# Two of the four weight sums of each feed-forward Strassen block made by accumulating DMA, and a third such block in ten of the eleven gate/up pairs

## What is computed

```python
def swiglu(h, w_gate, w_up, w_down):
    return (jax.nn.silu(h @ w_gate) * (h @ w_up)) @ w_down   # D_FF = 5632
x = x + swiglu(rmsnorm(x, norm_ffn_g), w_ffn_gate, w_ffn_up, w_ffn_down)
return rmsnorm(x, norm_final_g)
```

## Time and profile before

| | us |
|---|---|
| median of 3 runs | 1755.81 |
| lowest and highest | 1754.05, 1756.22 |
| the profiled execution, its time | 1754.56 |
| its span, first to last instruction | 1752.2 |
| feed-forward part, from about | 1035 |

### The profile page before, as it was taken

How to read it: one execution, slowest core, us unless ns; L and a number is a source line. 1 busy time by engine, 2 the same in 40 slices (tenths; PEclk the granted TensorE clock), 3 DMA queues, 4 the chain that set the end, 5 groups by cost and what they waited for, 6 DMA issues and landing times.

```text
span 1752.2 us, 20308 instructions
## 1 busy us (share of the span) xinstructions
PE 1740.3 (99%) x7926; PEld 1444.7 (82%) x7926; DVE 1283.2 (73%) x1399; ACT 972.8 (56%) x1209; POOL 28.4 (2%) x54
## 2 busy tenths in 40 slices
PE   9999999999999999999999999999999999999998
PEld 7888888888888888888888888888888888888886
DVE  7577677887575757655565578888888788888787
ACT  6767678554555555544455465555545545555554
POOL 1000000000000000000000000000000000000000
PEclk9999999999999999999999999999999999999999
DMA  8565665666565655556755455566666565666664
GB/s 284 173 200 167 204 193 162 199 204 204 163 209 168 216 168 189 172 186 209 249 184 189 138 177 181 192 194 194 196 209 207 184 209 192 192 192 194 215 202 158
DMA packets 176047, 338.22 MB, mean 193 GB/s; under 512 B 10704, under 2 KB 15312, under 8 KB 175696
## 3 DMA queue, kind: packets, MB, share of 16 engines
q1 hardware_dynamic: 173232, 327.72, 59.3%
q0 software_dynamic: 1296, 5.24, 0.9%
q10 hardware_dynamic: 1424, 3.97, 0.6%
HBM read 334.80 MB, written 2.10 MB: 192 GB/s over the span
## 4 chain that ended last, share of the span: by engine, by line
PE 97%; DVE 1%; ACT 0%; DMA 0%; issue 0%; ACTq 0%; DVEq 0%; POOLq 0%; POOL 0%
PE group L468 29%; PE group L470 29%; PE group L469 29%; PE side L468 2%; PE side L469 2%; PE side L470 2%; PE side L531 2%; DVE w_lo L1199 0%; DMA x_T_in<-in_x_T 0%; PE side L649 0%; PE side L633 0%; PE side L587 0%; PE side L586 0%; PE side L585 0%; DVE x_res L1551 0%
## 5 line engine op out<-in xcount | busy, mean ns | idle before, releaser
L817 ACT ACTIVATE w_hi<-w_raw 128x1024 fp32r<-128x1024 f32 x612 | 622.9, 1029 | 543.5 <-PE group L470 447.9
L1199 DVE TENSOR_TENSOR w_lo<-w_raw,w_hi 128x1024 fp32r<-128x1024 f32 x612 | 712.6, 1186 | 286.3 <-ACT w_hi L817 280.3
L468 PE MATMUL group<-w_hi,x_hi 128*128 128x512 f32 x1466 | 575.6, 393 | 0.5 <-DVE w_lo L1274 0.3
L470 PE MATMUL group<-w_hi,x_lo 128*128 128x512 f32 x1466 | 571.0, 390 | 0.0
L469 PE MATMUL group<-w_lo,x_hi 128*128 128x512 f32 x1466 | 570.5, 389 | 0.0
L468 PEld LDWEIGHTS group<-w_hi,x_hi 128*128 128x128 f32 x1466 | 275.3, 188 | 58.9 <-DVE w_lo L1199 2.0
L470 PEld LDWEIGHTS group<-w_hi,x_lo 128*128 128x128 f32 x1466 | 275.1, 188 | 57.9
L469 PEld LDWEIGHTS group<-w_lo,x_hi 128*128 128x128 f32 x1466 | 275.4, 188 | 55.6
L817 ACT ACTIVATE w_hi<-w_sums 128x1024 fp32r<-128x1024 f32 x84 | 89.1, 1061 | 148.1 <-PE group L470 107.2
L1199 DVE TENSOR_TENSOR w_lo<-w_sums,w_hi 128x1024 fp32r<-128x1024 f32 x84 | 102.5, 1223 | 56.5 <-ACT w_hi L817 56.4
L468 PE MATMUL group<-w_hi,v_hi 128*128 128x512 f32 x296 | 115.9, 392 | 0.0
(11 more groups left out here) (304 smaller groups left out, 1707.4 us busy)
## 6 DMA issues: line engine op xcount, KB each, us to landing
w_raw<-in_w_in SPq DMA_DIRECT2D x223, 512.0 KB, 4.2
w_raw<-in_w_ffn_gate SPq DMA_DIRECT2D x88, 512.0 KB, 4.0
w_raw<-in_w_ffn_up SPq DMA_DIRECT2D x88, 512.0 KB, 4.6
w_raw<-in_w_ffn_down SPq DMA_DIRECT2D x88, 512.0 KB, 4.8
w_raw<-in_w_rnn_proj SPq DMA_DIRECT2D x32, 512.0 KB, 4.6
w_raw<-in_w_attn_proj SPq DMA_DIRECT2D x32, 512.0 KB, 4.3
w_raw<-in_w_mix_out SPq DMA_DIRECT2D x32, 512.0 KB, 4.6
w_raw<-in_w_xkv SPq DMA_DIRECT2D x16, 512.0 KB, 3.8
```

Source lines behind the costliest of these rows:

```text
L468: nc.tensor.matmul(out, h, whi[:, s, k, :], start=start, stop=False)
L470: return nc.tensor.matmul(out, l, whi[:, s, k, :], start=False, stop=stop)
L817: nc.scalar.activation(whi[:, s, ks], src[:, ks], ACT.Copy).then_inc(hi_ready[s], 1)
L1199: V_.tensor_tensor(wlo[:, s, ks], src[:, ks], whi[:, s, ks].bitcast(F32), ALU.subtract).then_inc(w_ready[s], 1)
```

## The change

- `UP_PLAN`, used by ten of the eleven gate/up pairs, goes from two blocks (W3, W5) to three (W1, W3, W5). So the sums of x are made for three k pairs (`us`, `us_hi`, `us_lo`).
- In all blocks of the feed-forward part (`FED`: 31 of gate/up, 11 of down) L1214 goes. GpSimd feeds the two sums by DMA: one load writes the second weight's top tile into two tiles of `w_sums`; when it has landed, two accumulating loads add the first weight's top tile to one of them and the second weight's bottom tile to the other. Before it starts a feed it waits until C and D of the block before the last have been split and the feed before has landed. VectorE waits for the feed (`sums_fed`) in `weight_sums`.
- `w_sums` has six tiles: the two fed ones alternate between tiles 0, 2 and 4, 5. The tiles 1 and 3 of VectorE's own sums stay single. The room comes from laying the rotary tables over the two added tiles.
- The copy of P1 is made two steps sooner in all pairs. In the ten pairs with the new plan, where the last block ends three steps before the end instead of five, `fold_rest` starts at the D step instead of the one after.
- The blocks of the recurrent branch and of the keys (10) keep VectorE's sums.

```diff
-UP_PLAN = "O0 O1 W3 O2 O4 W5 O6 O7".split()
+UP_PLAN = "O0 O2 W1 O4 W3 O6 W5 O7".split()
...
+            def feed(first):
+                (w0, w1), row0, (col0, col1) = FFN[first]
+                for c, (kind, kp, _) in enumerate(STEPS[first]):
+                    if kind != "A":
+                        continue
+                    turn = TURN[N0[first] + c]
+                    if turn >= 2:
+                        before = FED[turn - 2]
+                    else:
+                        before = SUMMED["C"][SUM_OF[FED[0] + 2] - 2] - 2
+                    for n in (before + 2, before + 3):
+                        s, used = slot_of(n)
+                        pool.wait_ge(w_ready[s], START + used + 1)
+                    if turn:
+                        pool.wait_ge(sem("sums_fed"), 48 * turn)
+                    t1, t3 = ((0, 2), (4, 5))[turn % 2]
+                    row = row0 + kp * CK * P
+                    top, bottom = slice(row, row + P), slice(row + P, row + 2 * P)
+                    pool.dma_start(w_sums[:, t1:t3 + 1:t3 - t1, :], w1[top, col1:col1 + GW].unsqueeze(1).to_broadcast([P, 2, GW]))\
+                        .then_inc(sem("sums_fed"), 16)
+                    pool.wait_ge(sem("sums_fed"), 48 * turn + 16)
+                    pool.dma_start(w_sums[:, t1, :], w0[top, col0:col0 + GW], accum_op=ALU.add).then_inc(sem("sums_fed"), 16)
+                    pool.dma_start(w_sums[:, t3, :], w1[bottom, col1:col1 + GW], accum_op=ALU.add).then_inc(sem("sums_fed"), 16)
...
             root_of("x1")
+            feed(("gate_a", 0))
             root_of("x2")
+            for first in list(FFN)[1:-1]:
+                feed(first)
             pool.wait_ge(sem("inner_T"), FA + FB)
...
             pool.dma_start(gain_final[:, :], dram["norm_final_g"].partition_broadcast(P)).then_inc(sem("gain_final_loaded"), 16)
+            feed(list(FFN)[-1])
...
-                if last_sum(first) is not None and c == last_sum(first) + 1:
-                    wait_product(act, N0[first] + c)
+                if last_sum(first) is not None and c == last_sum(first) - 1:
+                    wait_product(act, N0[first] + c - 1)
...
-                then(V_.tensor_tensor(w_sums[:, :, 0, :], tiles[:, a:a + 4:3, :], tiles[:, a + 2:a + 3, :].to_broadcast([P, 2, GW]), ALU.add))
-                then(V_.tensor_tensor(w_sums[:, 1, 1, :], w_sums[:, 0, 0, :], tiles[:, a + 3, :], ALU.add))
+                t1 = 0
+                if m in TURN:
+                    dve.wait_ge(sem("sums_fed"), 48 * (TURN[m] + 1))
+                    t1 = (0, 4)[TURN[m] % 2]
+                else:
+                    then(V_.tensor_tensor(w_sums[:, 0:3:2, :], tiles[:, a:a + 4:3, :], tiles[:, a + 2:a + 3, :].to_broadcast([P, 2, GW]), ALU.add))
+                then(V_.tensor_tensor(w_sums[:, 3, :], w_sums[:, t1, :], tiles[:, a + 3, :], ALU.add))
                 dve.sem_inc(sem("sum_D"), 1)
-                V_.tensor_tensor(w_sums[:, 0, 1, :], w_sums[:, 1, 1, :], tiles[:, a + 1, :], ALU.add).then_inc(sem("sum_C"), 1)
+                V_.tensor_tensor(w_sums[:, 1, :], w_sums[:, 3, :], tiles[:, a + 1, :], ALU.add).then_inc(sem("sum_C"), 1)
...
                 at_, fold = last_sum(first), fold_of(first)
-                if at_ is not None and c == at_ + 1:
+                early = 1 if first[0].startswith(("gate", "up")) and at_ == len(STEPS[first]) - 3 else 0
+                if at_ is not None and c == at_ + 1 - early:
```

More of the change, by code:

```diff
@@ L136, in last_sum, with sum_tiles_of @@
     return len(kinds) - 1 - kinds[::-1].index("D") if "D" in kinds else None
+FED = [_n for _first, _second, _plan in PLACED if _second is not None and _first[0].startswith(("gate", "down"))
+       for _n in range(N0[_first], N0[_first] + len(STEPS[_first])) if KIND[_n] == "A"]
+TURN = {_n: _i for _i, _n in enumerate(FED)}
+def sum_tiles_of(m):
+    n = m - " ABCD".index(KIND[m]) + 1
+    if TURN.get(n, 0) % 2 == 0:
+        return {"C": slice(0, 2), "D": slice(2, 4)}[KIND[m]], (0, 1)
+    return {"C": slice(1, 5, 3), "D": slice(3, 6, 2)}[KIND[m]], (1, 0)
 LAST_HALVES = [slice(D - GW, D - GW // 2), slice(D - GW // 2, D)]
@@ L308, in wait_taken @@
             engine.wait_ge(taken[p], START + before + 1)
+        FFN = {}
+        for part, f0, groups in (("a", 0, FA), ("b", FA, FB)):
+            for j in range(groups):
+                FFN["gate_" + part, j] = (dram["w_ffn_gate"], dram["w_ffn_up"]), 0, ((f0 + j) * GW,) * 2
+            for q in range(0, KG, 2):
+                FFN["down_" + part, q] = (dram["w_ffn_down"],) * 2, f0 * GW, (q * GW, (q + 1) * GW)
         block = ctx.enter_context(nc.Block())
@@ L374, in _ @@
                 group(N0["cross_out", j], dram["w_xo"], j * GW, rows_=NB)
[L375 to L379, removed]
+            for first, (ws, row0, cols) in FFN.items():
+                pair(first, ws, row0, cols)
             for tt in range(TT):
@@ L517, in pair_of @@
                     if kind == "B":
-                        last = products(gps[p1][:, 0, :], sh[:, w, 3, :], sl[:, w, 3, :], s, 1, False, False)
+                        last = products(gps[p1][:, 0, :], sh[:, w, 3, :], sl[w][:, 3, :], s, 1, False, False)
                     if kind == "C":
-                        products(Q5, sh[:, w, 0, :], sl[:, w, 0, :], s, 0, begin, end)
-                        last = products(gps[p0][:, 1, :], xh[:, k1, tok1], xl[:, k1, tok1], s, 1, False, False)
+                        _, (i1, i4) = sum_tiles_of(N0[first] + c)
+                        products(Q5, sh[:, w, 0, :], sl[w][:, 0, :], s, i1, begin, end)
+                        last = products(gps[p0][:, 1, :], xh[:, k1, tok1], xl[:, k1, tok1], s, i4, False, False)
                     if kind == "D":
-                        products(P7, sh[:, w, 2, :], sl[:, w, 2, :], s, 0, begin, end)
-                        last = products(P6, sh[:, w, 1, :], sl[:, w, 1, :], s, 1, begin, end)
+                        _, (i3, i2) = sum_tiles_of(N0[first] + c)
+                        products(P7, sh[:, w, 2, :], sl[w][:, 2, :], s, i3, begin, end)
+                        last = products(P6, sh[:, w, 1, :], sl[w][:, 1, :], s, i2, begin, end)
                     last.then_inc(w_used[s], 1)
@@ L594, in _ @@
                 first = ("rnn_out", q)
-                for c, kind, kp in pair_of(first, vhi, vlo, xs_hi, xs_lo, R_SUMS):
+                for c, kind, kp in pair_of(first, vhi, vlo, xs_hi, (xs_lo[:, 0], xs_lo[:, 1]), R_SUMS):
                     if q == 0 and c == 0:
@@ L610, in _ @@
                     first = ("k", j)
-                    for c, kind, kp in pair_of(first, xhi, xlo, ks_hi, xs_lo, K_SUMS):
+                    for c, kind, kp in pair_of(first, xhi, xlo, ks_hi, (xs_lo[:, 0], xs_lo[:, 1]), K_SUMS):
                         if kind == "A" and kp == FIRST_SUM[first]:
@@ L749, in _ @@
                     first = ("gate_" + part, j)
-                    for c, kind, kp in pair_of(first, xhi, xlo, xs_hi, xs_lo, X_SUMS):
+                    for c, kind, kp in pair_of(first, xhi, xlo, us_hi, (us_lo[0][:, 0], us_lo[0][:, 1], us_lo[1][:, 0]), X_SUMS):
                         if c == 2 and (part, j) == ("a", 0):
@@ L767, in _ @@
                 for q in range(0, KG if part == "a" else KG // 2, 2):
-                    for c, kind, kp in pair_of(("down_" + part, q), inner_hi, inner_lo, fs_hi, fs_lo, F_SUMS[part]):
+                    for c, kind, kp in pair_of(("down_" + part, q), inner_hi, inner_lo, fs_hi, [fs_lo[:, w] for w in range(4)], F_SUMS[part]):
                         if c == 3 and q == 0:
@@ L781, in _ @@
             held = len(steps) - R
-            for c, kind, kp in pair_of(first, inner_hi, inner_lo, fs_hi, fs_lo, F_SUMS["b"], held):
+            for c, kind, kp in pair_of(first, inner_hi, inner_lo, fs_hi, [fs_lo[:, w] for w in range(4)], F_SUMS["b"], held):
                 if kind == "A" and kp == FIRST_SUM[first]:
@@ L1139, in _ @@
                             if c == 1:
-                                sums_hi(xs_hi[:, :, :, :], x_sum[:, :, :, :])
+                                sums_hi(us_hi[:, :, :, :], us[:, :, :, :])
                         if j > 0:
@@ L1196, in splits @@
                         ks = slice(1, 2) if KIND.get(m) == "B" else slice(0, CK)
-                        src = raw[:, raw_of(m)[0]] if m in LOAD_OF else w_sums[:, "CD".index(KIND[m])]
+                        src = raw[:, raw_of(m)[0]] if m in LOAD_OF else w_sums[:, sum_tiles_of(m)[0]]
                         dve.wait_ge(hi_ready[s], used + 1)
```

39 lines of the change are left out of this document (23 added, 16 removed).

## The result

| | us |
|---|---|
| the changed kernel, median of 4 runs | 1776.28 |
| lowest and highest | 1773.21, 1777.9 |
| the kernel before beside it, median of 4 runs | 1755.76 |
| ratio, 95% interval | 1.0119 (1.0107 to 1.0131) |
| the profiled execution, its time and its span | 1773.21, 1771.4 |

A forecast was written before the change was run, and what follows sets the result against it. TensorE's matmuls were taken to bound the kernel. The terms -6.8 (matmuls), -0.7 (a stall gone) and +1.0 (later weight loads) gave -6.5 us: 1748.1 profiled, 1749.3 as median; range 1747.3 to 1760.

The forecast's parts named there:

- at the pair's end, two chunks are left after the last sum instead of four: At the end of gate/up pairs, VectorE readies inner tokens 12.7 us after the last D, 13.6 allowed: slack 0.9, no cost.
- the fold starts one step sooner: At the pair's end, the earlier fold goes under ScalarE's split of the next chunk, where VectorE had waited; priced at nothing.
- the 1.0 us for crowding: In ten gate/up pairs, weight loads get later beside the feeds: 0.1 us a pair allowed, 1.0 in all.
- The share: DMA engines' share in a gate/up pair: from 0.61 to 0.85 at plain price, 0.97 with accumulating bytes counted twice.
- Rival 2: Weight loads crowded by feeds: 1751 to 1757 at third blocks and next pairs' third chunks, or 1778 if DMA-bound; chance 0.18.
- The matmuls: In ten gate/up pairs, 30 matmuls go, saving 6.8 us; the pair's period falls from 43.28 to 42.60.
- VectorE's load: Per gate/up pair, VectorE's work goes from 37.7 to 38.6 of 42.6 us, 91%, no bound on average.
- The slack of 0.5 at the second block's A: In gate/up pairs also summing inner activations, VectorE finishes the second A's split 0.5 to 0.6 us early; no cost.
- The 0.7 us stall of the earlier trace: In the last down pair, TensorE's delay behind VectorE's removed sum L1214 goes: 0.7 us saved.
- The feed window: At third blocks of gate/up pairs, feeds land within 12.8 us without waits, 15.2 without a stall; no stall priced.
- rival 1: Accumulating loads slow, stalling third blocks' sums in ten pairs once landing exceeds 9.0 us; 1766 at 10.8; chance 0.12.
- Rival 3: VectorE's order: slacks at the second A and pair's end become 0.3 to 0.7 us stalls a pair, 1751 to 1755; chance 0.08.

The follow-up runs named there:

- run 1: The changed kernel with the joins of the ten pairs moved ahead of splits, same work in another order: 1760.47 us, ratio 1.0026.
- join_first_plain: The changed kernel with joins moved ahead and each feed's two accumulating loads made plain loads of the same bytes: 1754.06 us, ratio 0.9994.
- run 10: The changed kernel with joins moved ahead and no feed, VectorE making all sums of every block: 1759.12 us, ratio 1.0021.
- run 8: The changed kernel with joins moved ahead and only the 31 gate/up blocks fed, VectorE summing for the down pairs: 1755.42 us, ratio 0.9998.
- run 5: The changed kernel with joins moved ahead and no feed transfers, the fed sums left as zeros: 1746.62 us, ratio 0.9947.

## Why the prediction was wrong

**The step that failed first: "at the pair's end, two chunks are left after the last sum instead of four".** There I walked VectorE's list to the inner tokens, found 0.9 us of slack and stopped. The same list frees the bank of `group` on its way, and TensorE wants that at the very first chunk of the next pair, long before its transposes. The walk itself had what was needed: a split (ends 1.45 after the D), two folds 1.4, a split 1.15, two folds 1.4, a join 1.15 is 6.6 us, against two chunks of 2.72, 5.4: 1.1 late. The trace has 1.31 with nothing else amiss. I compared the walk with one consumer and not with each. That "the fold starts one step sooner ... priced at nothing" belongs to it: the folds fill just the two steps in which the join is wanted. Price: 15.8 us beside the feeds (run 1), 14.0 beside tiny ones, 7.8 beside VectorE's sums, where fewer waits are left inside the pairs (3.6 us instead of 8.8). None of it was in the sum.

**The second step: the 1.0 us for crowding.** It measured 13.9 us by the medians, 12.3 in the traces. The share was right within its range. By the bytes I forecast 0.85 for plain feeds and 0.97 for accumulating ones; where nothing else lengthens a pair it is 0.81 in `join_first_plain` and 0.91 in `join_first`. "DMA: Bandwidth & Descriptors" of the Trainium skill (Rules for kernel authors) has an accumulating DMA read its destination and write it back; the 1.96 above agrees. What failed is the price of a late load. I asked whether a late weight tile reaches TensorE through the ring, and the earlier trace rows said no for one 2 MB load in 10 us. But a load that is late by 2.87 us, about one chunk's time, also delays VectorE, whose list holds more than splits, and in down pairs loads were late enough to reach TensorE. I had priced the third block of gate/up pairs alone, and the down pairs not at all. Rival 2 had crowding right and its place in part: two third blocks stall, for 0.48 and 0.58, some pairs lose nothing, and over half of the cost is in the down pairs. Its hard form, with the DMA engines themselves full at a share of 1.08, never came.

**What held.**
- The matmuls: 7896, and a period of 42.60 us where neither joins nor transfers disturb. Without crowding the sum is -7.5: in the traces the feed-forward part takes 702.1 instead of 709.9, 7.8 less. The medians have 8.9 less, 1746.6.
- VectorE's load: 38.3 us a pair, forecast 38.6.
- The slack of 0.5 at the second block's A: no gap there. The gaps of 0.60 without feeds (run 10) show how thin it is once 1.22 more is in the list.
- The 0.7 us stall of the earlier trace rows is gone, and the first pair, with the larger sums of x, has no gap.
- The feed window: the second accumulating load has 7.1 us (9.3 at most) against 9.0, and no block of gate/up waits for its feed in the changed kernel. With the joins ahead two do, for 2.1 us at most, and no gap comes of it; only run 8 has the stall that rival 1 describes, once. So rival 1 did not come about as put; slow these loads are, and they hurt others.
- Rival 3, VectorE's order, named the right resource but the wrong places and prices (0.3 to 0.7 a pair, against 1.31). It is the nearest to what decided.

**The sum again, by medians.** 1755.5 before; -8.9 for matmuls and stalls that go (run 5); +13.9 for the feeds, 7.4 bytes and 6.4 accumulating (runs 1, 5, 6); +15.8 for the late join on top of them: 1776.3. For the feed-forward part in the traces it is 709.9 - 7.8 + 12.3 + 15.2 = 729.6. The changed kernel's gaps there are 25.3 us more than those of run 5.

**Open.** What the sooner fold is worth alone: in the changed kernel's list the second half of the folds can't follow the join, which writes the same tile, so that wasn't tried. The sooner copy of P1 wasn't tried alone either; run 5 has it and shows no gap for it. Why the tiny transfers lengthen the end of the program. What the 6.4 us for accumulating come from, the bytes handled twice or the smaller packets. How little the late join's price depends on late loads is nearly settled: it is 14.0 by the medians and 14.9 in the traces beside tiny transfers, 15.8 and 15.2 beside full ones.

## What to carry to other kernels

When a step moves toward a boundary, list everyone that the engine's in-order list releases on the way, a PSUM bank above all, and compare each with its own deadline; the nearest deadline decides, not the last. Ahead of a boundary, put first what gives a bank back. Work moved from a 90% busy engine to the DMA engines is paid by the loads that share them: here 12.5 us of VectorE's cost were exchanged for 13.9, no gain within the noise, while half of the offload, and only in gate/up, was the best amount of those tried.

## What the chip showed that was not expected

- An accumulating load of 256 KB from GpSimd lands in 5.2 us, the second one issued behind it in 7.1, where plain ones take 4.1 and 5.1. It costs GpSimd more to issue as well, 0.86 and 1.18 us against 0.55 and 0.54, and has more packets (19440 against 14064 for the same 49.29 MB).
- After TensorE's pause of 2.8 us at 1122.91 the first five matmuls started at the 2.4 GHz pitch or near it and the next seven 0.43 us apart, which is 1.2 GHz; after the one of 3.3 us, at 1435.23, they were slow from the first on, six or seven of them. After the changed kernel's pauses of 1.3 to 2.3 us the pitch stayed that of 2.4.
- At a share of 0.87 to 0.88 for the DMA engines over whole pairs of the changed kernel, ScalarE waits up to 4.8 us for a weight tile of gate (1.7 before), though the median landing of up rises only from 4.6 to 5.4.
- Transfers of 16x32 in place of full ones made the program's end, behind the last VectorE instruction, 5.6 us longer.
